# Attention output of a one-core transformer layer: folding two halves on the tensor engine and scaling on the vector engine, instead of transposing and adding on two others

## What is computed

```python
def fox_attend(q, k, v, cq, ck, pos_q, pos_k):
    s = jnp.einsum('bqhd,bkhd->bhqk', q, k).astype(jnp.float32) * HEAD_DIM ** -0.5
    decay = jnp.transpose(cq, (0, 2, 1))[:, :, :, None] - jnp.transpose(ck, (0, 2, 1))[:, :, None, :]
    mask = pos_k[None, :] <= pos_q[:, None]
    s = jnp.where(mask[None, None], s + decay, NEG_INF)
    p = jax.nn.softmax(s, axis=-1)
    return jnp.einsum('bhqk,bkhd->bqhd', p.astype(v.dtype), v)
...
# per layer
z = rms(x, g_pre_mix) @ w_in                 # q | k | v | forget | B | C | u
mix = concat(rms(attention), rms(B * causal_conv3(C * u))) @ w_o
x = x + rms(mix, g_post_mix)
x = x + rms(relu(rms(x, g_pre_mlp) @ w_up)**2 @ w_down, g_post_mlp)
```

## Time and profile before

| | |
|---|---|
| median of 3 runs | 2926.05 us (2925.41 to 2933.53) |
| the profiled execution | 2925.41 us |
| its span, first to last instruction | 2923.8 us |
| mean granted PE clock | 0.978 |
| busy over the span: PE, PEld | 2766.0 us (95%), 2424.5 us (83%) |
| DVE, ACT, POOL | 1271.9 us (44%), 895.1 us (31%), 927.0 us (32%) |
| attention stage | about 648 to 1164 us |
| HBM traffic | 305.23 MB, 104 GB/s |

### The profile page before, as it was taken

The page is one execution under the profiler, slowest core; times in us unless marked ns, Lnnn a source line. Parts: engine busy times, 40 slices in busy tenths (PEclk is TensorE's granted clock), DMA queues, the critical chain, the costliest instruction groups (busy, mean ns, idle before and its releaser), DMA issues.

```text
span 2923.8 us, 40223 instructions
## 1 busy us (share of the span) xinstructions
PE 2766.0 (95%) x14550; PEld 2424.5 (83%) x14550; DVE 1271.9 (44%) x2362; ACT 895.1 (31%) x1621; POOL 927.0 (32%) x613
## 2 busy tenths in 40 slices
PE   7999999999898988799699999999999999999997
PEld 6899899987777777588599999999987888888886
DVE  4333343348786777577423223232235223222235
ACT  3201201127676766455211111212122121121122
POOL 3233334211111111444233333333245333333333
PEclk9999999999999999899899999999999999999999
DMA  6543535674433333566910111111146111111113
GB/s 180 183 125 116 159 104 157 197 186 120 104 94 93 94 93 94 164 210 208 259 57 30 57 43 43 43 43 43 43 130 197 59 44 48 53 43 56 44 43 115
DMA packets 261442, 305.23 MB, mean 104 GB/s; under 512 B 19324, under 2 KB 221704, under 8 KB 256712
## 3 DMA queue, kind: packets, MB, share of 16 engines
q1 hardware_dynamic: 209272, 256.14, 29.6%
q0 software_dynamic: 14304, 21.63, 2.9%
q10 hardware_dynamic: 37744, 25.96, 2.8%
HBM read 221.21 MB, written 82.21 MB: 104 GB/s over the span
## 4 chain that ended last, share of the span: by engine, by line
PE 46%; DMA 2%; POOL 2%; DVE 1%; ACT 0%; issue 0%; SPq 0%; POOLq 0%
PE up_bank L2340 23%; PE dn_bank L2363 23%; DMA m_x_in<-scratch_x 1%; DVE y L2294 1%; POOL y L2158 1%; DMA m_h_lo<-scratch_h_lo 0%; POOL dn_lo L2138 0%; POOL up_lo L2138 0%; DMA m_x_in<-y 0%; DMA m_raw<-in_w_down 0%; POOL u_hl L2150 0%; DVE y L2281 0%; POOL m_h_hi L2130 0%; DVE up_lo L2297 0%; ACT dn_hi L2209 0%; ACT up_hi L2209 0%
## 5 line engine op out<-in xcount | busy, mean ns | idle before, releaser
L2363 PE MATMUL dn_bank<-dn_hi,u_hl 128*128 128x512 f32 x2112 | 671.5, 390 | 6.9 <-DVE y L2279 4.4
L2150 POOL TENSOR_TENSOR u_hl<-u,u_hl 128x64 fp32r<-128x64 f32 (+2 forms) x192 | 200.2, 1066 | 900.7 <-DVE u L2266 900.7
L2363 PEld LDWEIGHTS dn_bank<-dn_hi,u_hl 128*128 128x128 f32 x2112 | 397.1, 188 | 90.7 <-DVE y L2279 4.8
L2340 PE MATMUL up_bank<-m_h_hi,up_hi 128*128 128x512 f32 (+2 forms) x1280 | 452.6, 354 | 17.1 <-DVE up_lo L2297 11.3
L2340 PE MATMUL up_bank<-m_h_lo,up_hi 128*128 128x512 f32 (+2 forms) x1280 | 451.9, 353 | 0.0
L2340 PE MATMUL up_bank<-m_h_hi,up_lo 128*128 128x512 f32 (+2 forms) x1280 | 451.9, 353 | 0.0
L2219 ACT ACTIVATE u<-up_bank 128x512 f32<-128x512 f32 (+2 forms) x160 | 83.7, 524 | 1159.8 <-PE up_bank L2340 1153.5
L2281 DVE TENSOR_TENSOR y<-dn_bank,y 128x1024 f32<-128x1024 f32 x255 | 312.0, 1224 | 289.2 <-PE dn_bank L2363 289.1
L2363 PE MATMUL dn_bank<-dn_lo,u_hl 128*128 128x512 f32 x1088 | 424.6, 390 | 0.0
L2266 DVE TENSOR_TENSOR u<-u 128x512 f32<-128x512 f32 (+2 forms) x160 | 93.9, 628 | 698.0 <-ACT u_hl L2222 698.0
L504 POOL TENSOR_TENSOR w_lo<-w_raw,w_hi 128x1024 fp32r<-128x1024 f32 x72 | 181.3, 2522 | 336.1 <-DVE w_hi L722 336.1
(11 more groups left out here) (256 smaller groups left out, 4828.0 us busy)
## 6 DMA issues: line engine op xcount, KB each, us to landing
w_raw<-in_w_in SPq DMA_DIRECT2D x72, 512.0 KB, 4.1
m_raw<-in_w_up SPq DMA_DIRECT2D x32, 1024.0 KB, 5.4
m_raw<-in_w_down SPq DMA_DIRECT2D x32, 1024.0 KB, 4.8
nck<-scratch_ncum SPq DMA_DIRECT2D x9, 1312.0 KB, 18.6
scratch_v_hl<-vhl SPq DMA_DIRECT2D x20, 512.0 KB, 2.6
q_hi<-scratch_q_hi SPq DMA_DIRECT2D x18, 528.0 KB, 7.6
q_lo<-scratch_q_lo SPq DMA_DIRECT2D x18, 528.0 KB, 9.4
v_hl<-scratch_v_hl SPq DMA_DIRECT2D x9, 1024.0 KB, 20.7
```

The costliest lines, as they stand in the source:

```text
L2150: rest = pool.tensor_tensor(u_hl[:, o % 2, b, to], u[:, b, at], u_hl[:, o % 2, b, at].bitcast(F32), ALU.subtract)
L2340: mm = pe.matmul(up_bank[2 * (o % 2) + b][:, 0:w], wp[:, c, k, b * P:(b + 1) * P], hp[g][s][:, k, :], start=(k == 0 and p == 0), stop=(k = ...
L2363: mm = pe.matmul(bank[:, cols], u_hl[:, o % 2, b, part], wp[:, c, b, cols], start=(b == 0 and p == 0), stop=(b == 1 and p == len(passes) - 1))
```

## The change

Step N is done another way. PE no longer transposes a block of `o_t`: it multiplies it, as the stationary operand, by `fold` (64 columns, fp32), which turns the block and adds its two halves at once, and `n_bank` gets 64 columns a block instead of 128. ACT's copy to `o_n` is gone, and so are POOL's add, multiply and store: POOL has no step in the loop any more. DVE, after its reciprocals, waits for PE's matmuls and multiplies `n_bank` by the reciprocals straight into `att`, which now has two buffers. SP issues the store of `att`, at N's place in SP's own list. Before DVE writes a buffer it waits until the store from that buffer two N steps back has landed.

```diff
-DELAY = {"act": {"M": 6, "T": 1, "O": 3, "N": 2}, "dve": {"M": 1, "T": 3}}
+DELAY = {"act": {"M": 6, "T": 1, "O": 3}, "dve": {"M": 1, "T": 3}}
...
-        att = sb("att", [P, 4, HD])
+        att = sb("att", [P, 2, 4, HD])
...
+                if x.kind == "N":                                   # SP
+                    sp.wait_ge(att_done, 1 + upto("N", it, x.at) + 1)
+                    sp.dma_start(dst..., att[rows, x.at % 2, 0:n, :]).then_inc(att_stored[x.at % 2], 16)
...
-                pool.wait_ge(n_taken, 1 + upto("N", it, x.at) + 1)
-                pool.tensor_tensor(att[:, 0:n, :], o_n[:, 0:n, 0, :], o_n[:, 0:n, 1, :], ALU.add).then_inc(added, 1)
-                pool.tensor_tensor(att[:, 0:n, :], att[:, 0:n, :], rtotal[...], ALU.mult).then_inc(att_done, 1)
-                pool.dma_start(dst..., att[rows, 0:n, :]).then_inc(att_stored, 16)
-                pool.wait_ge(att_stored, 16 * (upto("N", it, x.at) + 1))
...
-                    act.activation(o_n[:, 0:n]..., n_bank[:, 0:n * P], ACT.Copy).then_inc(n_taken, 1)
...
                     dve.reciprocal(rtotal[:, m:m + n], total[:, m:m + n]).then_inc(recip_done, 1)
+                    dve.wait_ge(recip_done, upto("N", it, x.at) + 1)
+                    dve.wait_ge(in_rows, 2 + upto("N", it, x.at) + 1)
+                    dve.wait_ge(att_stored[x.at % 2], 16 * (per["N"] // 2 * it + x.at // 2 + 1))
+                    dve.tensor_tensor(att[:, x.at % 2, 0:n, :], n_bank[:, 0:n * HD]..., rtotal[...], ALU.mult).then_inc(att_done, 1)
...
-                    pe.wait_ge(n_taken, upto("N", it, x.at) + 1)
+                    pe.wait_ge(att_done, upto("N", it, x.at) + 1)
                     for i in range(4 if x.g < EXTRA else 1):
-                        mm = pe.transpose(n_bank[:, i * P:(i + 1) * P], o_t[:, x.at % 2, i * P:(i + 1) * P], ident[:, :])
+                        mm = pe.matmul(n_bank[:, i * HD:(i + 1) * HD], o_t[:, x.at % 2, i * P:(i + 1) * P], fold[:, :], start=True, stop=True)
```

More of the change, by code:

```diff
@@ L1199, in attend @@
         o_t = sb("o_t", [P, 2, 512])
-        o_n = sb("o_n", [P, 4, 2, HD])
-        att = sb("att", [P, 4, HD])
-        ident_r, mask_r = pre.ident_r, pre.mask_r
+        att = sb("att", [P, 2, 4, HD])
+        fold, ident_r, mask_r = pre.fold, pre.ident_r, pre.mask_r
         maxes = sb("maxes", [P, 34, 4])
@@ L1223, in attend @@
         o_taken = sem("o_taken")
-        in_rows, n_taken, added = sem("in_rows"), sem("n_taken"), sem("added")
+        in_rows = sem("in_rows")
         recip_done = sem("recip_done")
         att_done = sem("att_done")
-        att_stored = sem("att_stored")
+        att_stored = [sem(f"att_stored{i}") for i in range(2)]
         before, body, start, per = attention_order()
@@ L1265, in step @@
             def step(it, x):
+                if x.kind == "N":
+                    rows = slice(0, P) if x.g < EXTRA else slice(0, DEC)
+                    n = 4 if x.g < EXTRA else 1
+                    sp.wait_ge(att_done, 1 + upto("N", it, x.at) + 1)
+                    dst = dr["attn"][x.g * 4 * P:(x.g * 4 + n) * P, :] if n == 4 else dr["attn"][SEQ:ROWS, :]
+                    sp.dma_start(dst.rearrange("(a p) (i c) -> p a i c", a=n, c=2 * HD)[:, :, it, x.off * HD:(x.off + 1) * HD],
+                                 att[rows, x.at % 2, 0:n, :]).then_inc(att_stored[x.at % 2], 16)
                 if x.kind != "L":
@@ L1273, in step @@
                 load_values(sp, dr, h, v_hl[x.par], v_loaded[x.par])
+            for i in range(2):
+                sp.sem_inc(att_stored[i], 16)
             loop(sp, "sync", step)
+            for i in range(2):
+                sp.wait_ge(att_stored[i], 16 * (1 + per["N"] // 2 * (HEADS // 2)))
             sp.wait_ge(qk_loaded[0], 96 * (HEADS // 2 + 1))
@@ L1282, in _ @@
         def _(pool):
-            pool.sem_inc(added, 1)
             pool.memset(q_hi[1][:, ROWS:].bitcast(F32), 0.0)
@@ L1288, in _ @@
                 pool.sem_clear(s)
[L1290 to L1295, removed]
-                pool.wait_ge(n_taken, 1 + upto("N", it, x.at) + 1)
-                pool.tensor_tensor(att[:, 0:n, :], o_n[:, 0:n, 0, :], o_n[:, 0:n, 1, :], ALU.add).then_inc(added, 1)
[L1298 to L1305, removed]
-                pool.wait_ge(att_stored, 16 * (upto("N", it, x.at) + 1))
-            loop(pool, "pool", step)
         @block.scalar
@@ L1312, in _ @@
             act.sem_inc(o_taken, O_BANKS)
-            act.sem_inc(n_taken, 1)
             def step(it, x):
@@ L1329, in step @@
                     act.activation(o_t[:, x.at % 2, 0:width], o_bank[x.at % O_BANKS][:, 0:width], ACT.Copy).then_inc(o_taken, 1)
[L1331 to L1335, removed]
             loop(act, "act", step)
@@ L1342, in _ @@
             dve.sem_inc(lo_done, T_BANKS)
+            dve.sem_inc(att_done, 1)
             pieces = dve.alloc_register("pieces")
@@ L1373, in step @@
                     dve.reciprocal(rtotal[:, m:m + n], total[:, m:m + n]).then_inc(recip_done, 1)
+                    dve.wait_ge(recip_done, upto("N", it, x.at) + 1)
+                    dve.wait_ge(in_rows, 2 + upto("N", it, x.at) + 1)
+                    dve.wait_ge(att_stored[x.at % 2], 16 * (per["N"] // 2 * it + x.at // 2 + 1))
+                    dve.tensor_tensor(att[:, x.at % 2, 0:n, :], n_bank[:, 0:n * HD].rearrange("p (a d) -> p a d", d=HD),
+                                      rtotal[:, m:m + n].rearrange("p (a o) -> p a o", o=1).to_broadcast([P, n, HD]), ALU.mult).then_inc(att_done, 1)
             loop(dve, "dve", step)
```

## The result

| | before | changed | ratio, 95% interval |
|---|---|---|---|
| median | 2925.73 us (4 runs) | 2957.38 us (4 runs, 2956.86 to 2960.93) | 1.0107 (1.0086 to 1.0129) |
| the profiled execution | 2925.41 us | 2960.39 us | |
| its span | 2923.8 us | 2958.7 us | |

The changed kernel is 31.6 us slower by the medians, and 35.0 us between the two profiled executions; the one of the changed kernel lies 3.0 us above its median. The forecast was +45 us, 2970, in a range of 2934 to 2995. Where the traces are compared, the sum is of the two profiled executions (35.0 us of device time, 34.9 of span).

What follows compares the result with a forecast made beforehand. The attention stage was taken as a ring, PE to ACT to DVE to PE, with no engine full. Terms 15 - 1 + 34 + 4 - 2 - 3 - 1.8 gave +45 on 2925.4: 2970 us, range 2934 to 2995.

Steps and rivals of the forecast that it cites:

- The store behind the loads: Mid-turn, N4's store queues behind SP's loads, so DVE stands still at N6 in four turns: +34 us, bounds 23 to 40.
- The restart, +4 and slack, -2: After each N6 stall PE restarts at half clock, +1 us each, bounds 0 and 8; slack there returns 0.5 us each.
- PE's second pair: Step N on PE: two pairs of weight load and matmul a block instead of one, +15 us, bounds 8 to 24.
- Rival F: Step N on PE: four pairs a block instead of two, 30 us more, 3000 us; chance 0.02.
- DVE's multiply, counted with PE's: DVE's multiply at N, about 0.45 us each, 16 us in all, runs beside PE's delay; only the larger is counted.
- ACT and POOL relieved: Step N: ACT's 40 copies leave it idle instead; only its four waits for POOL are credited, -1 us; POOL's share 0.
- rival D: Attention stage: ACT sets the ring's pace, so its 40 removed copies make the kernel faster, 2903 us; chance 0.06.
- The jump back: Loop's backward jump, three times: ACT may gain, DVE may lose; -1 us each, -3 us, bounds -15 and +6.
- One of the prediction's own signs of being wrong: At the jump back: the prediction is wrong if ACT's pause is gone, being worth more than the forecast gives it.
- The end of the stage: From PE's last N to the next stage's first load: 4.8 us instead of 6.6, so -1.8 us.
- B: The stall at N6 does not come and only the work is added: 2935 us; chance 0.10.
- E: A second stall each turn, at N2, waiting for N0's store behind the other loads: 24 us more, 2994; chance 0.04.

Runs made afterwards that it cites:

- e1: The changed kernel with five buffers of `att` instead of two, stores still in SP's queue: 2927.28 us, ratio to before 1.0012.
- e3: The changed kernel with the L step (loads) 13 places later in SP's list, behind N4's store: 2937.51 us, ratio to before 1.0049.
- e8: The changed kernel with one buffer of `att`, so each N waits for the store just before it: 3022.05 us, ratio to before 1.033.
- e4: The kernel before with only PE's matmul by `fold`; ACT still copies (half the columns), POOL still multiplies and stores: 2935.03 us, ratio 1.0036.
- e5: e1 with `o_t` and `fold` rounded to fp32r, one pair a block, low output bits left out: 2916.20 us, ratio to before 0.9973.
- e2: The changed kernel, two buffers, but POOL issues the store on its own queue, waits for its landing and signals DVE: 2948.03 us, ratio to before 1.0076.
- e6: The kernel before, with SP holding back the loads (L) at the turn's start until ACT has copied N9: 2907.44 us, ratio 0.9937.
- e7: e2 with the loads (L) at the turn's start held back until DVE's multiply of N9: 2933.38 us, ratio to before 1.002.
- e9: The kernel before with only the store moved to SP, with five buffers of `att`: 2904.05 us, ratio 0.9932.

## Why the prediction was right, and where its terms were off

The direction and the mechanism were right, and the time was in the range; the size was 10 us too high against the profiled execution and 13 us against the median.

- **The store behind the loads, +34.** Right, in place, cause and size: four waits of DVE at N6, 34.5 us. The terms beneath it were each off by a little and against each other: the store lands 27.2 us after L's start (28.9 forecast), and N6's turn is at 19.2 (19.4). e1, e3 and e8 show the cause by taking the wait away, moving it and doubling it.
- **The restart, +4 and slack, -2.** Mis-sized. The stretch N6 to N7 is 36.4 us longer, of which 34.5 are the waits and 1.3 remain in e1, where there is no wait. That leaves 0.6 us for both. PE does restart at the lower clock (0.50 granted, 0.79 us for its first 512-column matmul), but it costs nothing behind: N7 to N8 is 17.6 us in the changed kernel and in e1. That DVE has the filled banks to work through meanwhile is an argument; no run tests it.
- **PE's second pair, +15.** Two pairs, as the rows said: 272 records, 0.84 us an N. The Trainium skill ("FP8 and Floating Point Precision", TensorE Precision Notes) has true FP32 in four passes through the array. Rival F counted each pass as a pair, and that is out; whether a pair holds more than one pass, no run shows. The term was too high, since it was taken in all ten steps of a turn: in place it is 6.6 to 6.9 us in the long stretches. The medians of e4 (10.6 us) and e5 (11.1 us) are higher, but part of e4's is at the jumps.
- **DVE's multiply, counted with PE's.** Right in the main: 0.425 us at the median, hidden in the dense groups (17.6 us with it in e1 and without it in e4). Wrong in one group of each head, where DVE is the fuller and it adds 0.4 to 0.5 us.
- **ACT and POOL relieved, -1.** Right that they bring next to nothing: the dense groups don't get shorter with the copies gone. They are 17.2 us with the copies (before) and without them (e5), both with one pair a block, and 17.6 us with half copies (e4) and without (e1), both with two. So rival D is out.
- **The jump back, -3.** The step that was least understood. It was -5.4 us, in the bounds; but it was booked as ACT leaving its turn earlier. One of the prediction's own signs of being wrong came true here: ACT's unexplained pause at the jump is gone. It was worth less than feared, since PE now pauses 2.9 us and ACT waits for PE, as long as it stood before. That -3 was near -5.4 is luck. e2, e6 and e7 show that what counts is whether an engine jumps before or after L's loads begin. The change gained there because N9's store holds L back, and lost part of it again, because DVE and PE now leave the turn late and pause 3 us themselves (in e1, where DVE alone pauses, 2.7 to 3.1 us, the stretch is 15.1 to 16.1 us, in e6 11.9 to 12.2).
- **The end of the stage, -1.8.** -2.4 us.
- Not foreseen: -2.5 us ahead of the attention and -1.7 us behind it. The first comes and goes by itself: in e6 and e9, whose programs are the kernel before up to there, the first N0 is at 653.4 and 653.2, and in e5 and e8 at 655.8 and 655.4. The second no run explains; the kernel before varies by 20 us from run to run (2916.6 to 2936.2), and it may be no more than that.

The forecast was 10 us above the profiled execution mainly because of PE's term, these 4.2 us, the jump and the restart.

Of the rivals, B's case is what e1 makes of the change once the stall is gone: 2927 us, B said 2935. The gap of some 8 us is in the main B's two terms that were off, PE's (15 instead of 7 in the long stretches) and the jump (-3 instead of -7.9 in e1), less DVE's 3 us in one group of each head, which B didn't have. E is out: DVE waits for no store at N2.

## What to carry to other kernels

A store that is moved to an engine that "has nothing to do" takes its place in that engine's queue: look at how long the longest issue ahead of it holds that queue (here up to 18 us inside one DMA instruction), and give the tile buffers enough to outlast it, or leave the queue. Two buffers are enough only if a store lands before the second step behind it needs its buffer. And look at the loop's seam: which engine jumps back while big loads run; one wait that held the loads back by some 2 us was worth 17 us here.

## What the runs showed of the hardware that was not expected

- An engine's pause at the backward jump of the loop depends on the DMA traffic. ACT: 6.79 us, with loads since 2 us, and 2.13 us with loads that began 0.2 us behind its last instruction (e6). DVE: 7.51 us with loads since 2 us (e2), 3.12 us with the loads behind it (e1). The DMA view supports that the pause is the fetching of instructions behind the loads: the long pauses end with two packets on an instruction queue, over 4.4 us behind the engine's last instruction, and in e6 the two come within 0.9 us. The view doesn't say for which engine a packet is, so this last link is a reading.
- POOL's stores passed beside the same loads, on another queue, and landed at most 9.9 us after their issue (e2). SP's store of N4 landed 4.1 us after its own issue, but that came 23.1 us after L's start. So the other queue is slowed, but it isn't held. That SP stands in L98 because its queue is full is a reading; the rows show the 18 us.
- A plain fp32 matmul with 128x128 stationary and 64 moved columns costs two pairs of 0.105 us (0.84 us for eight), that is as much as two fp32 transposes of 128 columns (0.11 us each).
